# Layer 2's attention in steps between quarter slabs of the last gate and the first output group

## The reference, cut to what matters

```python
h = rmsnorm(x, norm_gain)
q_a, k_a, v_a, z_a, c_q, c_kv, k_rope, z_b = split(h @ w_in_2)    # 512,512,512,512,256,128,32,512 columns
o_a = dilated_window_attention(rmsnorm(q_a), rmsnorm(k_a), v_a, rel_bias)   # 8 heads of 64
q = rmsnorm(c_q) @ w_uq;  kv = rmsnorm(c_kv) @ w_ukv              # 8 heads, 64 + 32 (rope) and 64 + 64
o_b = causal attention(rmsnorm(q) with rope, rmsnorm(k_nope) | rope(rmsnorm(k_rope)), v)
x = x + concat(o_a * silu(z_a), o_b * silu(z_b)) @ w_out
```

## Time and profile before

| | us |
|---|---|
| median of 3 runs | 1025.78 |
| lowest, highest | 1021.7, 1028.36 |
| span of the profiled execution | 1020.2 |
| its mean granted TensorE clock | 0.979 of full |
| TensorE busy | 969.3 (95%), 5116 matmuls |
| DVE, ACT, POOL busy | 447.3, 444.3, 501.2 |

### The profile page before, as it was taken

How to read it: one execution, slowest core, us unless ns; L and a number is a source line. 1 busy time by engine, 2 the same in 40 slices (tenths; PEclk the granted TensorE clock), 3 DMA queues, 4 the chain that set the end, 5 groups by cost and what they waited for, 6 DMA issues and landing times.

```text
span 1020.2 us, 14034 instructions
## 1 busy us (share of the span) xinstructions
PE 969.3 (95%) x5116; PEld 791.5 (78%) x5116; DVE 447.3 (44%) x1062; ACT 444.3 (44%) x992; POOL 501.2 (49%) x476
## 2 busy tenths in 40 slices
PE   6999989999999999999999999999999988999998
PEld 5777788876888878777767877789778766778886
DVE  3300468224113432756564423325543268758811
ACT  5333553334224344555456422236335325748721
POOL 3543544534445744654544444443654664845543
PEclk9999999999999999999999999999999997959999
DMA  6332211322223222222111241222322311100022
GB/s 211 103 98 69 83 42 33 93 65 100 94 92 104 83 83 83 63 62 63 48 57 46 79 165 63 103 82 79 107 85 80 112 45 59 37 27 1 1 84 103
DMA packets 41171, 78.76 MB, mean 77 GB/s; under 512 B 3296, under 2 KB 5088, under 8 KB 41104
## 3 DMA queue, kind: packets, MB, share of 16 engines
q1 hardware_dynamic: 41104, 77.87, 24.3%
HBM read 75.74 MB, written 2.12 MB: 76 GB/s over the span
## 4 chain that ended last, share of the span: by engine, by line
PE 73%; DVE 10%; ACT 6%; issue 5%; POOL 5%; DMA 1%; SPq 1%; ACTq 0%; DVEq 0%; POOLq 0%
PE Z L1584 22%; PE Z L1586 21%; PE Z L1585 21%; POOL w_lo L819 2%; PE A L1584 2%; PE A L1716 2%; PE A L1586 1%; PE A L1585 1%; PE A L1594 1%; ACT prob L707 1%; PE A L1806 1%; DMA raw<-in_w_in 1%; PE A L1742 1%; ACT w_hi L491 1%; DVE m_sb L1134 1%
## 5 line engine op out<-in xcount | busy, mean ns | idle before, releaser
L819 POOL TENSOR_TENSOR w_lo<-raw,w_hi 128x512 fp32r<-128x512 f32 (+2 forms) x262 | 343.5, 1318 | 403.8 <-ACT w_hi L491 403.4
L1584 PE MATMUL Z<-w_hi,hT_hi 128*128 128x512 f32 (+1 forms) x832 | 334.4, 402 | 11.6 <-POOL w_lo L819 4.0
L1586 PE MATMUL Z<-w_hi,hT_lo 128*128 128x512 f32 (+1 forms) x832 | 323.9, 389 | 0.0
L1585 PE MATMUL Z<-w_lo,hT_hi 128*128 128x512 f32 (+1 forms) x832 | 323.3, 389 | 0.0
L491 ACT CAST w_hi<-raw 128x512 fp32r<-128x512 f32 (+2 forms) x262 | 158.0, 615 | 273.1 <-PE Z L1586 258.3
L1584 PEld LDWEIGHTS Z<-w_hi,hT_hi 128*128 128x128 f32 x832 | 156.3, 188 | 52.3 <-POOL w_lo L819 6.4
L1586 PEld LDWEIGHTS Z<-w_hi,hT_lo 128*128 128x128 f32 x832 | 156.2, 188 | 33.0
L1585 PEld LDWEIGHTS Z<-w_lo,hT_hi 128*128 128x128 f32 x832 | 156.6, 188 | 27.4
L1584 PE MATMUL Z<-w_hi,oT_hi 128*128 128x512 f32 x128 | 51.6, 403 | 3.3 <-DVE tmp L1119 2.2
L955 POOL TENSOR_SCALAR prob<-prob,rinv 128x128 f32<-128x128 f32 (+1 forms) x64 | 34.0, 532 | 33.7 <-DVE rinv L1400 31.9
L1586 PE MATMUL Z<-w_hi,oT_lo 128*128 128x512 f32 x128 | 50.1, 391 | 0.0
(11 more groups left out here) (288 smaller groups left out, 1674.9 us busy)
## 6 DMA issues: line engine op xcount, KB each, us to landing
raw<-in_w_in SPq DMA_DIRECT2D x92, 512.0 KB, 3.5
raw<-in_w_out SPq DMA_DIRECT2D x16, 512.0 KB, 3.7
raw<-in_ret_w_o SPq DMA_DIRECT2D x8, 512.0 KB, 3.5
raw<-in_diff_w_o SPq DMA_DIRECT2D x8, 512.0 KB, 3.5
x_sb<-in_x SPq DMA_DIRECT2D x8, 256.0 KB, 5.1
x_sb<-in_x SPq DMA_DIRECT2D x4, 512.0 KB, 6.6
bias<-bias_dram SPq DMA_DIRECT2D x8, 256.0 KB, 3.2
out<-x_sb SPq DMA_DIRECT2D x8, 256.0 KB, 4.0
```

Of the source, the lines that this page charges most:

```text
L819: pool.tensor_tensor(w_lo[:, s % SPLIT_SLOTS, 0:width], raw[:, c % RAW_SLOTS, s - CHUNK_START[c], 0:width], w_hi[:, s % SPLIT_SLOTS, 0:wid ...
L1584: pe.matmul(out, l_hi, r_hi, start=first, stop=False)
L1585: pe.matmul(out, l_hi, r_lo, start=False, stop=False)
L1586: return pe.matmul(out, l_lo, r_hi, start=False, stop=last)
```

## The change

- The values' group of layer 2 (`w_in_2` from 1024) moves behind w_ukv_2 and is now group 31. The gates stay 32 and 33, the outputs 34 and 35.
- The attention has 69 steps, done between the quarter slabs of groups 33 and 34: after quarter v (0 to 63) as many as `att_due` says, 36 in the first 31 quarters, 3 at quarter 31, one after each up to quarter 56, the last five after 57 to 59.
- As Z is taken by the groups, scores have only A[0], turned weights only A[2], outputs only A[3], turned queries and keys only A[1], queries in one step and keys in the next. Waits are for the set before, not for the one before that.
- In each step TensorE does outputs, turn, queries or keys, then the next scores. DVE does queries' or keys' low part, then `pT_lo` (n - 3), then the maxima (n), and the gate of a head one step after its last output.
- A head is multiplied into its gate in place. Pairs 0 to 3 are split late (0 and 1 at the end of group 33, 2 and 3 at the beginning of 34), because `hT` is the operand of group 33 till then; pairs 4 to 7 in steps 44, 52, 60 and 68.
- The gates of group 33 are taken at its slab 7, one tile ahead of each quarter's steps (`take_gates` is a generator now).
- The squares use a part of `sgd_sb` instead of `bias`; key and query squares, latent norms and query norms are done within groups 31 and 32. SP loads the first two biases at group 31; ACT issues the other six in steps.

```diff
+ATT_STEPS, ATT_FIRST = 69, 39
+def att_due(v):
+    if v < 0:
+        return 0
+    if v < 31:
+        return 36 * (v + 1) // 31
+    if v < 56:
+        return ATT_FIRST + (v - 31)
+    return min(ATT_STEPS, 64 + 2 * (v - 56))
...
         def score_bank(ph, n, j):
-            return (A[0], Z[0])[n % 2]
+            return A[0]
         def turn_bank(ph, n):
-            return A[2] if n % 2 == 0 else A[1]
+            return A[2]
...
@@ ACT, in the step @@
                         act.copy(pT_hi[:, m % 2, 0:wm], turn_bank(ph, m)[:, 0:wm]).then_inc(p_hi, 1)
                     if n < N:
...
+                        if i == 3 and h + 2 < H:
+                            act.dma_start(bias[:, h % 2, :], dilated_bias(h + 2)).then_inc(dil_in[h % 2], 16)
-                    if i == 1 and starts_job(ph, h + 1):
-                        qk(job_of(ph, h + 1))
+                    if i < 2 and starts_job(ph, h + 1):
+                        att_qk(job_of(ph, h + 1), i)
                     if i == 0 and 1 <= h < 2 * H:
-                        values(h)
+                        att_values(h)
+                    if n >= 8 * 4 + 12 and n % 8 == 4:
+                        split_pair((n - 12) // 8)
+                    yield
+            def att_slot(g, k, steps):
+                v = TT * (KD * (g - G_ATT2) + k)
+                hi(SLAB0[g] + k + 3)
+                for t in range(TT):
+                    if k == KD - 1:
+                        take(g, t)
+                    if g == G_ATT2 and k == KD - 1 and t == TT - 1:
+                        split_pair(0)
+                        split_pair(1)
+                    if g == G_OUT2 and k == 0 and t < 2:
+                        split_pair(2 + t)
+                    for _ in range(att_due(v + t) - att_due(v + t - 1)):
+                        next(steps)
...
 @@ DVE, in the step @@
-                for n in range(N + 8):
+                for n in range(ATT_STEPS):
                     h, i = divmod(n, 4)
-                    if n < N:
-                        scores(n)
-                    if 1 <= n <= 4:
-                        query_norms(n - 1)
+                    if i in (1, 2) and starts_job(ph, h + 1):
+                        att_qk(job_of(ph, h + 1), i - 1)
                     if 0 <= n - LAG - 1 < N:
                         m = n - LAG - 1
                         wm = P * (m % 4 + 1)
                         dve.wait_ge(p_hi, ph["n0"] + m + 1)
                         dve.tensor_tensor(pT_lo[:, m % 2, 0:wm], turn_bank(ph, m)[:, 0:wm], pT_hi[:, m % 2, 0:wm],
                                           ALU.subtract).then_inc(p_lo, 1)
+                    if n < N:
+                        scores(n)
...
+                    if i == 3 and h >= 1:
+                        hd = h - 1
                         p = hd // 2
                         dve.wait_ge(o_mm, ph["n0"] + 4 * hd + 4)
+                        gate = gateT[e * (hd % 2):e * (hd % 2 + 1), p, :]
+                        dve.tensor_tensor(gate, A[3][0:e, :], gate, ALU.mult).then_inc(head_gated, 1)
+                    yield
+            def att_slot(g, k, steps, gates):
+                v = TT * (KD * (g - G_ATT2) + k)
+                for t in range(TT):
+                    if g == G_ATT2 and k == KD - 1 or g == G_OUT2 and k == 0 and t == 0:
+                        next(gates)
+                    if g == G_OUT2 and k == KD - 1:
+                        take(g, t)
+                    for _ in range(att_due(v + t) - att_due(v + t - 1)):
+                        next(steps)
...
 @@ TensorE @@
-                    if n >= 2:
-                        pe.wait_ge(s_max, set_count(ph, n - 2) + 1)
+                    if n >= 1:
+                        pe.wait_ge(s_max, set_count(ph, n - 1) + 1)
...
-                    pe.wait_ge(p_lo, ph["n0"] + m - 1)
+                    pe.wait_ge(p_lo, ph["n0"] + m)
...
                 scores(0)
-                for n in range(N + LAG + 2):
+                for n in range(ATT_STEPS):
                     h, i = divmod(n, 4)
-                    if n + 1 < N:
-                        scores(n + 1)
...
-                    if n >= LAG + 2:
+                    if 0 <= n - LAG - 2 < N:
                         outputs(n - LAG - 2)
                     if 0 <= n - LAG < N:
                         turn_probs(n - LAG)
+                    if i < 2 and starts_job(ph, h + 1):
+                        if h + 1 == H:
+                            pe.wait_ge(q_latent, 1)
+                        att_qk(job_of(ph, h + 1), i)
+                    if n + 1 < N:
+                        scores(n + 1)
+                    yield
...
+                        if in_att(g):
+                            v = TT * (KD * (g - G_ATT2) + k) + t
+                            for _ in range(att_due(v) - att_due(v - 1)):
+                                next(steps2)
...
                 if g == G_ATT2:
-                    pe.wait_ge(z_by_dve, dve_evacs[G_OUT2])
-                    attention()
-                    pe.wait_ge(s_max, set_count(ATT2, 8 * H))
```

More of the change, by code:

```diff
@@ L737, in _ @@
             act.activation(cols[:, 35:36], cols_in[:, 35:36], ACT.Copy, scale=DK ** -0.5)
-            steps = diff()
+            steps, steps2 = diff(), attention()
             for g in range(NG + 1):
                 n = NK[g] if g < NG else 0
-                for k in range(0 if g and in_diff(g - 1) else min(n, 2)):
+                for k in range(0 if g and in_steps(g - 1) else min(n, 2)):
                     if g == 0:
@@ L794, in _ @@
                         retention(k // 2 - 1)
-                    if k == START_SLAB and g == G_ATT2:
-                        attention(start=True)
                     if g + 1 in EARLY and k >= 4:
@@ L992, in _ @@
                     continue
-                if g and g - 1 == G_ATT2:
-                    attention()
+                if in_att(g):
+                    for k in range(KD):
+                        att_slot(g, k, steps2)
+                    continue
                 for k in range(3, n):
@@ L1517, in _ @@
                         diff_slot(g, k, steps, norms)
+                    continue
+                if in_att(g):
+                    for k in range(KD):
+                        att_slot(g, k, steps2, gates)
                     continue
@@ L1571, in _ @@
                     latent_norms()
-                if g == G_ATT2:
-                    attention()
+                    for part in range(4):
+                        query_norms(part)
                 if g in HEAD_NORM:
-                    head_norm(HEAD_NORM[g])
+                    head_norm(HEAD_NORM[g], bias if g < G_LAYER2 else squares2)
         @block.tensor
```

274 lines of the change are left out of this document (136 added, 138 removed).

## The result

The changed kernel takes 1058.32 us (median of four runs, 1053.68 to 1062.58), the kernel before 1023.74 on the same chip: a ratio of 1.0317, with an interval of 1.0261 to 1.0373. The profiled execution spans 1051.8 us, where that of before spans 1020.2. The forecast was 1041, with a range of 1011 to 1062 (1036 to 1050 for the forecast's own story): the direction is right, the loss is twice the forecast.

The account below looks back on a forecast made before the run. TensorE, busy 95%, bounds the kernel, with some 33 us lost to waits and low clock within reach. Stage pieces sum to 212.6 us against 202.4, 10.2 more; 5 for the clock makes 15 on the median 1025.8: 1041 us, range 1011 to 1062.

Parts of the forecast that it names:

- gate group 1 with its wait: First gate group with the first job's transposes, 22.6 us, plus 1.5 us of TensorE waiting for qT_lo behind the norms.
- beginning, steps 0 to 31: 4.6 us wait at the start, then 79 us of 64-row heads, 10.7 with a job to turn, 9.1 without.
- steps 32 to 38 with gates: Steps at slab 7 of the second gate group, last gates ahead of each quarter's steps: 24.6 us.
- end: Steps 64 to 68, three quarters, pair 7's product and split, and slab 7 of the output group: 11.3 us.
- clock: Loss to low clock from the beginning's wait and the gates' waits, nearer case with quarters between: 5 us, bounds 0 and 15.
- the new 4.6 us wait: At the beginning, TensorE waits for the maxima of set 0, which stand behind the first group's gates in DVE's order.
- The main term: Each attention step: maxima, exp, pT_hi, pT_lo close a loop of one step instead of two, 7.7 us a head.
- My laid-out head: A 96-row head followed step by step through the queues: ends at 10.5 us, where TensorE's own work is 9.7.
- The quarter alone: Quarter slabs standing singly between steps: 0.83 us each against 0.68 (bounds 0.79 and 0.89), 9 us more in all.
- The loop did not hide: Rival: the steps' loop hides under TensorE's own work, stage 187 us, 15 us less, 1011 us; chance 0.15.
- It did not even out: Rival: step waits as laid out, but clock holds or beginning or gates cost half; 1031 us; chance 0.28.
- The clock's rival: Rival: clock falls and stays at 1.2 GHz in a third of the steps, 31 us more, 1062 us; chance 0.12.

Follow-up runs that it names:

- one kernel without quarters: Changed kernel with no quarter slabs between the attention's steps (43 steps after the second gate group, 26 in the output group): 1091.1 us, ratio 1.0604.
- the other kernel without quarters: Changed kernel without quarters between the steps and with the transposes of q and k first in TensorE's step: 1067.8 us, ratio 1.0438.
- three edits and filled waits: Changed kernel with transposes first, last gates behind steps, query norms in VectorE's first four steps, unread matmuls ahead of qT_lo and set 0's maxima: 1034.27 us, ratio 1.0076.

## Why the prediction was half right

Piece by piece, in the prediction's own terms (us, stage only):

| | predicted | measured | of it lost to the clock |
|---|---|---|---|
| gate group 1 with its wait | 24.1 | 31.3 | 3.4 |
| beginning, steps 0 to 31 | 83.6 | 88.5 | 8.5 |
| steps 32 to 38 with gates | 24.6 | 32.6 | 10.1 |
| steps 39 to 63 | 69 | 66.6 | 0 |
| end | 11.3 | 12.0 | 0.8 |
| clock | 5 | in the rows | 22.8 |
| stage | 217.6 | 231.1 | |

**The clock is the mis-sized term.** I let its loss shrink from 17 us to 5, with 15 as the upper bound; it grew, from 18.7 to 22.8. That is 17.8 us more than the sum had; without it the pieces are 4.3 us below it; 2.9 us lie ahead of the stage. 17.8 - 4.3 + 2.9 = 16.4, the gap between +15.2 and +31.6. I had reasoned that quarters between the steps hold the clock up. From 875 to 914 and from 946 to 1013 it does stay at 1.00 over waits in most steps, and in one kernel without quarters it was at 1.2 GHz for 88 us. But the other kernel without quarters held 1.00 over most of its 64-row heads, and the one with three edits and filled waits fell to 1.2 GHz with quarters in place: whether quarters hold the clock up isn't shown. I had also named the new 4.6 us wait and the gates' four waits as of the kind that brings it down, and priced them as if quarters between them undid that. Behind a wait of 6.2 us and one of 2.5 it was low for most of 22 us, slabs and quarters or not. The split is arithmetic only; the filled waits show that about half of such a loss comes back as time, so the 17.8 us are worth some 9 of time by that measure, an estimate, and the other 9 belong to waits that a slow TensorE covers.

**The wait of gate group 1** was 6.2 instead of 1.5 us. The work behind the last query square took 812.97 to 819.28, 6.3 us, where I had 6. What failed was the lead: I had the last square two slabs (5.5 us) ahead of TensorE, and it ended at 812.9, 1.0 us ahead of 813.97. GpSimd, which makes the squares, had waited for sums of VectorE twice, 4.9 us up to 790.75 and 2.4 us up to 802.47; that this is the cause no run tests. Moving the norms away gave 3.6 us in the stage.

**The main term was right in size and wrong in its mechanism.** 10.5 us for a 96-row head, and 0.57 for a split: measured 10.78 and 11.30. For 64 rows, 10.7 and 9.1: 9.4 to 10.6 at full clock. 79 + 69 us of steps were forecast with no clock loss, and 80 and 66.6 came. But the loop that I named, through the maxima, is not what closes: with the maxima first nothing is gained. My laid-out head had the true chain in it (transposes issued late, their copy ahead of pT_hi, pT_lo, the only bank), and the summary above it blamed the order in VectorE's queue. That summary's 7.7 us a head is also 8.1 by its own terms (7.5 and 16 hops of 0.04); the forecast doesn't use it. Single banks cost 20 us in the kernel before, and late transposes 12 in the changed one.

**The quarter alone**, 0.83 us by my choice against 0.68, took 0.68 to 0.75 in 96-row steps and about 0.80 in 64-row steps. It didn't matter: 0.9 us a pair of 96-row heads is all that eight quarters add, since the step waits anyway. The 9 us priced for it were part of heads which the chain set.

**Gates among the steps:** the chain is the one forecast, link by link, and 22.5 us without clock loss stand beside 24.6. Its fall of the clock (10 us) was the dear part; behind the steps the gates cost 9 us less.

**Beginning and end.** The start's wait was 2.5 us and not 4.6, because TensorE itself was slow then; at full clock 4.37 us of filling and 0.24 of waiting stood there, 4.6 together. The end took 12.0 against 11.3, with the 2.0 us wait for hT_lo as laid out. Bias loads and scaling on GpSimd cost nothing, as forecast.

**The rivals.** The loop did not hide (heads of 9.7 us or less were its mark; 10.8 came). It did not even out. The clock's rival, 1062 us, came nearest in time, but not as told: the clock did not fall and stay in a third of the steps, it fell mainly in two places behind long waits and came back. Its 1062 is also counted from the profiled 1020.2, where the forecast's 1041 is counted from the median of 1025.8; on the same footing it is 1067.

The Trainium skill (TensorE: Matmul & The Clock Gate, HAM oscillation — how this bites in real kernels) counts half of the time at the low clock as extra wall time. Here that holds as an upper bound only: 11.9 us of such penalty taken away gave 5.9. The same section found no gain from double-buffering PSUM in its kernel; here, where three engines take turns on the bank, going from two banks to one cost 20 us. Its next section (A second HAM failure mode: psum-queue depth-cycling) has small idles between groups swing the clock; the steps from 946 to 1013, with TensorE busy 85% and waits in most, at 1.00, do not show it. The fall from 864 on in the kernel with three edits and filled waits came right behind waits of 0.9 and 0.2 us, so the rule isn't refuted either.

## What to carry to other kernels

Before work is interleaved with a chain of small steps, measure the chain alone in its new form: here the filling cost 0.1 to 0.24 us a quarter and gave back 17 us, and giving up the second banks that it occupied cost 20. In an in-order queue, look at what a copy stands behind, and issue first whatever that needs; one place in TensorE's order was worth 12 us. Put long work that waits for a large group (here the gates, and the norms) behind the steps and not ahead of them, and price a wait of TensorE by what the clock does after it too.

## What the runs showed of the hardware

- The clock fell during an idle of 6.2 us and, with a second one of 2.5, was at 1.2 GHz for most of 22 us of slabs and quarters; with both filled it stayed at 1.00.
- 64-row steps alone ran at 1.2 GHz for 88 us with TensorE busy 98%; in the same kernel, 96-row steps with TensorE busy 65% (951 to 971 us: 13.07 of 20) ran at 1.00. With quarters between them the 64-row steps of the changed kernel ran at 1.00 from 875 to 914. But so did those of the other kernel without quarters from 868 to 912, with TensorE busy 82%, and in the kernel with three edits and filled waits they fell to 0.57 (864 to 884) with quarters between them. So neither the quarters nor the 64 rows alone decide.
- The time of an execution goes with its clock: the kernel with three edits and filled waits took 1024.0 us at a mean clock of 0.995 and 1038.4 at 0.982. What makes it fall around the fourth head stays open.
- A lower clock costs less than it seems where TensorE waits for others: 5.9 us came back of 11.9, about half here.
